# A first layer's opening with its modulation loaded, computed and used in two halves of the channels

## The reference, cut to what matters

```python
mod_l = (silu(c) @ w_mod[l] + b_mod[l])[:, None, :]
mod_c = (silu(c_ctx) @ w_mod[l] + b_mod[l])[None, None, :]
sh1, sc1, g1, sh2, sc2, g2 = split(mod_l, 6, axis=-1)
sh1c, sc1c, ... = split(mod_c, 6, axis=-1)
pl = _modulate(_rmsnorm(xl, norm1_w[l]), sh1, sc1) @ w_in[l]      # h * (1 + sc1) + sh1, then the projection
pc = _modulate(_rmsnorm(xc, norm1_w[l]), sh1c, sc1c) @ w_in[l]
```

## Time and profile before

| | |
|---|---|
| median of 3 runs | 3009.11 us (3007.6 to 3009.39) |
| profiled execution, its time | 3008.7 us |
| profiled execution, its span | 3006.9 us |
| TensorE busy | 2977.1 us (99%), 17179 matmul records |
| VectorE, ScalarE, GpSimd busy | 1657.6, 1048.0, 2075.4 us |
| mean granted TensorE clock | 0.999 of full speed |

### The profile page before, as it was taken

How to read it: one execution, slowest core, us unless ns; L and a number is a source line. 1 busy time by engine, 2 the same in 40 slices (tenths; PEclk the granted TensorE clock), 3 DMA queues, 4 the chain that set the end, 5 groups by cost and what they waited for, 6 DMA issues and landing times.

```text
span 3006.9 us, 49161 instructions
## 1 busy us (share of the span) xinstructions
PE 2977.1 (99%) x17179; PEld 2584.9 (86%) x17179; DVE 1657.6 (55%) x2214; ACT 1048.0 (35%) x1846; POOL 2075.4 (69%) x1583
## 2 busy tenths in 40 slices
PE   7999999999999999999999999999999999999999
PEld 5878978888889988887889998899888878899987
DVE  5753365889178742364347662577523652477631
ACT  4362153121146620232017650366301320166600
POOL 3614575888778887654777887788876546778874
PEclk9999999999999999999999999999999999999999
DMA  5202262322333333331223333333334313333332
GB/s 222 88 29 63 73 236 71 99 98 80 96 99 103 112 89 107 116 106 64 90 98 99 104 97 96 100 107 102 95 96 136 99 56 98 98 99 98 107 90 83
DMA packets 323100, 300.60 MB, mean 100 GB/s; under 512 B 6652, under 2 KB 316924, under 8 KB 319264
## 3 DMA queue, kind: packets, MB, share of 16 engines
q1 hardware_dynamic: 319056, 290.55, 30.5%
q10 hardware_dynamic: 3920, 8.36, 1.0%
HBM read 292.60 MB, written 2.10 MB: 98 GB/s over the span
## 4 chain that ended last, share of the span: by engine, by line
PE 96%; DVE 1%; DMA 1%; ACT 1%; issue 1%; SPq 0%; DVEq 0%; ACTq 0%
PE pm L2641 16%; PE pm L2643 16%; PE pm L2642 16%; PE pm L2770 8%; PE pm L2771 8%; PE pm L2772 8%; PE pa L2641 2%; PE pa L2643 2%; PE pa L2642 2%; PE pm L2720 1%; PE pm L2721 1%; PE pm L2722 1%; PE pm L3041 1%; DMA modraw<-in_w_mod 1%; PE pm L2671 1%; PE pa L3084 1%
## 5 line engine op out<-in xcount | busy, mean ns | idle before, releaser
L776 POOL TENSOR_TENSOR wlo<-raw,whi 128x512 fp32r<-128x512 f32 (+1 forms) x784 | 977.2, 1278 | 16.4
L772 POOL TENSOR_SCALAR whi<-raw 128x2048 fp32r<-128x2048 f32 (+1 forms) x196 | 336.5, 1717 | 699.8 <-PE pm L2643 326.5
L2641 PE MATMUL pm<-hh,whi 128*128 128x512 f32 x1064 | 421.2, 396 | 2.2 <-DVE sil L2408 2.2
L2643 PE MATMUL pm<-hh,wlo 128*128 128x512 f32 x1064 | 414.3, 389 | 0.0
L2642 PE MATMUL pm<-hl,whi 128*128 128x512 f32 x1064 | 414.3, 389 | 0.0
L794 POOL TENSOR_TENSOR wlo<-raw,whi 128x512 fp32r<-128x512 f32 x216 | 288.2, 1335 | 58.6 <-ACT whi L1445 41.1
L2770 PE MATMUL pm<-tsets,whi 128*128 128x256 f32 x1152 | 326.0, 283 | 0.0
L2771 PE MATMUL pm<-tsets,whi 128*128 128x256 f32 x1152 | 326.0, 283 | 0.0
L2772 PE MATMUL pm<-tsets,wlo 128*128 128x256 f32 x1152 | 326.0, 283 | 0.0
L2641 PE MATMUL pm<-uh,whi 128*128 128x512 f32 x836 | 325.4, 389 | 0.0
L2642 PE MATMUL pm<-ul,whi 128*128 128x512 f32 x836 | 325.2, 389 | 0.0
(11 more groups left out here) (549 smaller groups left out, 6755.0 us busy)
## 6 DMA issues: line engine op xcount, KB each, us to landing
raw<-in_w_ffn SPq DMA_DIRECT2D x88, 1024.0 KB, 5.3
raw<-in_w_in SPq DMA_DIRECT2D x61, 1024.0 KB, 5.1
raw<-in_w_ffn SPq DMA_DIRECT2D x64, 704.0 KB, 4.6
raw<-in_w_up SPq DMA_DIRECT2D x22, 1024.0 KB, 5.1
raw<-in_w_out SPq DMA_DIRECT2D x12, 1024.0 KB, 5.1
raw<-in_w_down SPq DMA_DIRECT2D x16, 704.0 KB, 4.6
modbuf<-in_w_mod SPq DMA_DIRECT2D x10, 1024.0 KB, 5.6
modraw<-in_w_mod SPq DMA_DIRECT2D x8, 1024.0 KB, 19.7
```

Of the source, the lines that this page charges most:

```text
L772: nc.gpsimd.tensor_scalar(h, r, 1.0, 1.0, ALU.mult, ALU.mult).then_inc(hi_done, 1)
L776: last = nc.gpsimd.tensor_tensor(o[:, c], r[:, c], h[:, c].bitcast(F32), ALU.subtract)
L2641: nc.tensor.matmul(out, wh, ah, start=start, stop=False)
L2643: return nc.tensor.matmul(out, wl, ah, start=False, stop=stop)
```

## The change

The modulation's first 2048 columns are loaded in two halves. The first holds groups 0 and 2, which are shift and scale of channels 0 to 511 (tiles 0 to 3), the second groups 1 and 3. The half of a tile's load is 0.5 MB, in runs of 512 columns (2 KB) where a load before had rows of 2048 columns (8 KB). `w_first` is loaded in two halves too, tiles 0 to 3 and tiles 4 to 7. The order of the transfers is now `col`, `ident`, `x`, six first halves, first half of `w_first`, two first halves, `cx`, eight second halves, second half of `w_first`, and slab 1 without a wait. One place moves: `modraw7` lies in `whi1` where it lay in `hl`.

TensorE does groups 0 and 2 of all eight tiles (`modulation_half`), four fillers, a turn of these groups, five fillers, and slab 0's products of tiles 0 to 3. Then groups 1 and 3 of all eight tiles, with the square sum of `cx` after the sixth, their turn, and slab 0's products of tiles 4 to 7. The eight fillers ahead of the first step stay; there are none around the second turn. ScalarE copies the sums of two groups at a time, each group's 32 rows by an instruction of its own, and squares `cx` only behind `hh` of tile 3. VectorE makes bias, scales, unrounded values and `hl` of tiles 0 to 3 first, then normalizes the other four tiles and adds up the squares of `cx`, and then does the second half. `modrow` is set to zero once by GpSimd.

```diff
-MOD_GROUP = (0, 0, 0, 0, 1, 1, 2, 3)
+MOD_GROUP = (0, 0, 0, 0, 0, 0, 1, 1, 2, 2, 2, 2, 2, 2, 3, 3)
+FIRST_GROUP, FIRST_K = 1, 4
...
+def mod_arrivals(b):
+
+    return 16 * (MOD_GROUP.count(b) + (b == FIRST_GROUP))
...
+            wm = io["w_mod"][0].rearrange("(k p) n -> k p n", p=P)
+
+            def mod_columns_of(half, k):
+
+                for_half = [a.rearrange("p (e h c) -> p h e c", e=2, h=2)[:, half] for a in (modraw[k][:], wm[k][:, 0:MOD_W])]
+                sp.dma_start(*for_half).then_inc(mod_loaded[MOD_GROUP[KD * half + k]], 16)
+
+            first_w = raw[0][:].rearrange("p k n -> p (k n)")
+            for k in range(KD):
+                if k == KD - 2:
+                    sp.dma_start(first_w[:, 0:FIRST_K * SLAB], io["w_first"][:, 0:FIRST_K * SLAB]).then_inc(mod_loaded[FIRST_GROUP], 16)
+                mod_columns_of(0, k)
             sp.dma_start(cx[:].rearrange("p k t -> p (k t)"), io["ctxT"]).then_inc(ctx_loaded, 16)
-
-            wm = io["w_mod"][0].rearrange("(k p) n -> k p n", p=P)
             for k in range(KD):
-                sp.dma_start(modraw[k][:], wm[k][:, 0:MOD_W]).then_inc(mod_loaded[MOD_GROUP[k]], 16)
-            sp.dma_start(raw[0][:].rearrange("p k n -> p (k n)"), io["w_first"]).then_inc(raw_loaded[0], 16)
+                mod_columns_of(1, k)
+            sp.dma_start(first_w[:, FIRST_K * SLAB:], io["w_first"][:, FIRST_K * SLAB:]).then_inc(raw_loaded[0], 16)
...
-                if i == 1:
-                    sp.wait_ge(raw_loaded[0], 16)
...
-                pool.wait_ge(raw_loaded[0], 16)
+                pool.wait_ge(mod_loaded[FIRST_GROUP], mod_arrivals(FIRST_GROUP))
                 for i, (k0, k1) in enumerate(FIRST_PIECES):
+                    if k0 == FIRST_K:
+                        pool.wait_ge(raw_loaded[0], 16)
...
+                squares(0)
+                roots(0)
+                act.wait_ge(mod_step, 2)
+                for g in (0, 2):
+                    rows = slice(32 * g, 32 * g + 32)
+                    nc.scalar.activation(modrow[0][rows, :], pm[1][rows, 0, :], ACT.Copy).then_inc(mod_step, 1)
+                act.wait_ge(mod_done, 3)
+                highs(0, 0, FIRST_K)
+                squares(1)
+                act.wait_ge(mod_used, KD)
+                for g in (1, 3):
+                    rows = slice(32 * g, 32 * g + 32)
+                    nc.scalar.activation(modrow[0][rows, :], pm[1][rows, 0, :], ACT.Copy).then_inc(mod_step if g == 1 else mod_row, 1)
+                roots(1)
+                act.wait_ge(mod_done, 6)
+                highs(0, FIRST_K, KD)
+                act.wait_ge(hn_done, KD // 2)
+                highs(1, 0, KD)
...
+                square_sums(0)
+                normalized(0, 0, FIRST_K)
+                v.wait_ge(mod_step, 5)
+                mod_columns_made(0)
+                lows(0, 0, FIRST_K)
+                normalized(0, FIRST_K, KD)
+                square_sums(1)
+                v.wait_ge(mod_turned, 1)
+                mod_columns_made(1)
+                v.sem_inc(pm_free[1], 1)
+                lows(0, FIRST_K, KD)
+                normalized(1, 0, KD)
+                lows(1, 0, KD)
...
-                    for g in range(4):
+                    for g in range(4) if i >= KD else (1, 3):
                         last = nc.tensor.matmul(out[32 * g:32 * g + 32, :], silc[:, k, :], src[:, T * g:T * g + T], start=k == 0, stop=k == KD - 1)
...
+            def modulation_half():
+
+                for k in range(KD):
+                    pe.wait_ge(mod_loaded[MOD_GROUP[k]], mod_arrivals(MOD_GROUP[k]))
+                    for g in (0, 2):
+                        last = nc.tensor.matmul(pm[1][32 * g:32 * g + 32, 0, :], silc[:, k, :], modraw[k][:, T * g:T * g + T], start=k == 0, stop=k == KD - 1)
+                last.then_inc(mod_step, 1)
+
+            def half_turn(half, bank, done):
+
+                which = ident[:].rearrange("p (g c) -> p g c", g=4)[:, half::2, 0:2]
+                for t in range(4):
+                    last = nc.tensor.matmul(bank[:, 8 * t:8 * t + 8].rearrange("p (g j) -> p g j", g=4)[:, half::2, :], modrow[0][:, P * t:P * t + P], which, start=True, stop=True)
+                last.then_inc(done, 1)
...
                 square_sum(0, std, T)
                 idle(8)
-                pe.wait_ge(mod_in, 1)
+                pe.wait_ge(mod_step, 1)
+                modulation_half()
+                idle(4)
+                pe.wait_ge(mod_step, 4)
+                half_turn(0, pm[1][:, 1, :], mod_step)
+                idle(5)
+                slab_opening(0, FIRST_K)
                 for k, _ in enumerate(modulation(0, KD)):
-                    if k == 3:
+                    if k == 5:
                         square_sum(1, rstd, CT)
-                    if k == 6:
-                        idle(4)
+                pe.wait_ge(mod_step, 6)
                 pe.wait_ge(mod_row, 1)
-                mod_turn(modrow[0], pm[1][:, 1, :])
-                idle(5)
+                half_turn(1, pm[1][:, 1, :], mod_turned)
```

More of the change, by code:

```diff
@@ L196, in build @@
         TILE = 4 * T
-        modraw = [place(f"modraw{k}", [P, MOD_W], F32, arena + (12 + 4 * k) * TILE if k < 7 else raw_at - 8 * TILE) for k in range(KD)]
+        modraw = [place(f"modraw{k}", [P, MOD_W], F32, arena + (12 + 4 * k) * TILE if k < 7 else raw_at + 12 * TILE) for k in range(KD)]
         uh = place("uh", [P, KF, T], F32R)
@@ L1033, in first, with squares @@
                 nc.scalar.preload_act_table_set("natural_log_exp_and_others")
-                for n, (src, loaded, w) in enumerate(((x, x_loaded, T), (cx, ctx_loaded, CT))):
+                def squares(n):
+                    src, loaded, w = ((x, x_loaded, T), (cx, ctx_loaded, CT))[n]
                     act.wait_ge(loaded, 16)
@@ L1040, in first, with roots @@
                         nc.scalar.activation(sqs[m % 4][:, 0:w], src[:, k, :], ACT.Square).then_inc(sq_done, 1)
-                for n, (acc, w) in enumerate(((std, T), (rstd, CT))):
+                def roots(n):
+                    acc, w = ((std, T), (rstd, CT))[n]
                     act.wait_ge(sq_summed, n + 1)
@@ L1045, in first, with highs @@
                     nc.scalar.activation(pa[n][:, 0:w], acc[:, 0:w], ACT.Exp, scale=-0.5).then_inc(rstd_done, 1)
[L1046 to L1053, removed]
+                def highs(n, k0, k1):
+                    src, hi, w = ((xn, hh, T), (cx, ch, CT))[n]
+                    for k in range(k0, k1):
+                        act.wait_ge(xn_done, KD * n + k + 1)
                         nc.scalar.activation(hi[:, k, :], src[:, k, :], ACT.Identity, bias=mod_col(0, k, n), scale=wsc[:, n, k:k + 1]).then_inc(hh_done, 1)
@@ L2044, in first, with square_sums @@
                 lower_bounds()
-                for n, (acc, w) in enumerate(((std, T), (rstd, CT))):
+                def square_sums(n):
+                    acc, w = ((std, T), (rstd, CT))[n]
                     for k in range(KD):
@@ L2054, in first, with normalized @@
                             nc.vector.tensor_copy(acc[:, 0:w], sqs[m % 4][:, 0:w]).then_inc(sq_added, 1)
-                for n, (src, dst, w) in enumerate(((x, xn, T), (cx, cx, CT))):
+                def normalized(n, k0, k1):
+                    src, dst, w = ((x, xn, T), (cx, cx, CT))[n]
                     v.wait_ge(rstd_done, n + 1)
-                    for k in range(KD):
+                    for k in range(k0, k1):
                         nc.vector.tensor_tensor(dst[:, k, :], src[:, k, :], pa[n][:, 0:w], ALU.mult).then_inc(xn_done, 1)
-                v.wait_ge(mod_turned, 1)
@@ L2061, in first @@
[L2061 to L2073, removed]
+                def mod_columns_made(half):
+                    to, bias = mod_turned_to(0)
+                    turned = mod_columns(pm[1][:, 1, :])
+                    raised = pm[1][:, 1, 4 * MOD_TILES1:5 * MOD_TILES1]
+                    at, scaled, ks = slice(half, half + 1), slice(2 + half, 3 + half), slice(FIRST_K * half, FIRST_K * half + FIRST_K)
+                    nc.vector.tensor_tensor(raised.rearrange("p (j g t) -> p t g j", g=2, t=4)[:, :, at, :], turned[:, :, scaled, :], bias[:, :, scaled, :], ALU.add).then_inc(mod_done, 1)
+                    nc.vector.tensor_tensor(to[:, :, at, :], turned[:, :, at, :], bias[:, :, at, :], ALU.add).then_inc(mod_done, 1)
+                    v.wait_ge(mod_done, 3 * half + 2)
+                    gain = cols("norm1", 0, KD).rearrange("p (o k) -> p o k", o=1)[:, :, ks].to_broadcast([P, 2, FIRST_K])
+                    nc.vector.scalar_tensor_tensor(wsc[:, 0:2, ks], raised.rearrange("p (j k) -> p j k", j=2)[:, :, ks], 1.0, gain, ALU.add, ALU.mult).then_inc(mod_done, 1)
+                    v.wait_ge(mod_done, 3 * half + 3)
@@ L2074, in first, with lows @@
+                def lows(n, k0, k1):
+                    src, hi, lo, w = ((xn, hh, hl, T), (cx, ch, cl, CT))[n]
+                    v.wait_ge(xn_done, KD * n + k1)
```

(11 more changed lines are left out.)

16 lines of the change are left out of this document (9 added, 7 removed).

## The result

The changed kernel takes 3017.36 us (median of 9 runs, 3016.7 to 3019.02) against 3008.76 for the kernel before (9 runs, 3007.35 to 3009.52): the ratio is 1.003, with a 95% interval of 1.002 to 1.004. The forecast was 3017.3. The profiled execution has a span of 3015.6 us, 8.7 more than before.

The account below looks back on a forecast made before the run. It took TensorE's matmul stream behind a serial opening as the bound, so slab 0's end counts: +6.5 us plus 1.7 for a clock drop, +8.2 on 3009.1, gives 3017.3 us; range 3012.5 to 3020.5.

Parts of the forecast that it names:

- eight steps with two groups: TensorE's first modulation half: a two-group step lasts 0.86 us like one with four, 7.05 us plus 0.25.
- slab 0 done, one drop of the clock: First projection's slab 0 ends 8.2 us later: +6.5 us, plus 1.7 for one clock drop behind the second turn; chance 50%.
- convolution starts on VectorE: VectorE reaches the convolution at 64.3 us, before its operands are needed at 69.
- the in-order wait of the second half: TensorE starts the second modulation half at 40.1 us, after tiles 0 to 3's products, though data landed at 35 to 38.
- the serial tail counted twice: Copies 1.25, turn 1.1, VectorE 0.5 and first `hh` 0.95 us recur after the second half, 47.9 to 51.7.
- The 0.25 us for a slow start of the steps: Time added to the first eight modulation steps on TensorE for the slower clock at their start.
- It just fits: VectorE's context square sums end at 45.2 us, when TensorE's sixth second-half step ends at 45.3, so no wait.
- two drops of the clock and none: Rival A: both turns lose the clock, 3019.0 us, chance 15%; or neither does, 3015.6 us, chance 12%.
- D: Rival: slab 2's bank or the context operands are late, TensorE waits 1 to 3 us more: 3018 to 3020; chance 8%.
- the 1 us of the sum: Slack for slab 2's bank: the convolution's first set ends at 74.1 us, slab 1 is through at 75 to 77.
- B: Rival: a two-group modulation step takes 0.43 us, half of four; 3011.3 to 3013.0 us; chance 12%.
- C: Rival: the opening follows its loads, slab 0 ends at 48.3 us, 2.4 us faster: 3006.7; chance 3%.

Follow-up runs that it names:

- the experiment with four groups: The changed kernel with its second half computing all four column groups again, twice the matmuls: 3018.01 us.
- the run with all edits: The changed kernel with two channel tiles per step, `x` normalized before the first turn, later context square sum, five fillers behind the second turn, four ahead: 3005.17 us.
- three more fillers: The kernel before with three more filler matmuls between the last modulation step and the turn: 3007.50 us.
- the run with two tiles to a step: The changed kernel with even and odd channel tiles in neighbouring column groups, all four working in both halves, the turn adding the sums: 3014.92 us.
- the run with half loads: The kernel before with each of the eight modulation loads issued as two transfers of half the columns, 2 KB runs: 3009.49 us.

## Why the prediction was right

The time was 3017.36 us where 3017.3 was said, and the range held it. The steps one by one, forecast and profile:

| step | forecast us | profile after us |
|---|---|---|
| first modulation step | 23.55 | 22.88 |
| eight steps with two groups | 7.05 + 0.25 | 7.06 |
| first product | 34.7 | 33.77 |
| second block of steps | 40.1 | 39.42 |
| square sum of the context | 45.3, no wait | 45.92, after a wait of 1.16 |
| last step done | 47.9 | 48.5 |
| first product of tile 4 | 51.7 | 52.35 |
| slab 0 done, one drop of the clock | 58.8 | 59.58 |
| convolution starts on VectorE | 64.3 | 64.64 |

The step that carries the result, that a step with two column groups lasts as long as one with four, held to 0.01 us over eight steps, and the experiment with four groups shows it apart from all else. So did the in-order wait of the second half, the serial tail counted twice, and the one drop of the clock. Several terms were off and partly offset each other:

- The first step came 0.7 us earlier. The fillers took 2.58 us and not 3.62. The fence below this list, from the view by tile, gives the minimum, median and maximum of their records in ns, first for the kernel before and then for the changed one. The granted clock reads 1.00 in both stretches, so the rows do not say why the pace differs. It is no effect of the change: with the same fillers this part took from 2.46 to 3.62 us in the variants' profiles.
- The 0.25 us for a slow start of the steps did not come.
- The context's sums took 5.7 us and not 4.0: their durations came from a stretch in which GpSimd stood idle, and here it did not. "It just fits" was the step that was wrong, mis-sized by the wait of 1.2 us.
- Four tiles' products took 5.65 us each time at the full clock and not 5.4, and the drop 1.6 and not 1.7.
- SyncE had not issued everything by 11.65 us, which was the reason given for its costing nothing: with twice the transfers its last issue of this group ends at 28.25. It cost nothing even so, since the data of tiles 4 to 7 were there at 38.5, within the forecast's 36 to 39.3.

```profile
L3209 PE MATMUL pm<-ident x16: 421/421/422, 19.9 to 23.1; 128*128 128x128 f32 x16
L3290 PE MATMUL pm<-ident x16: 275/275/421, 20.4 to 22.7; 128*128 128x128 f32 x16
```

The whole is 8.9 us at slab 0, 8.7 in the span and 8.6 in the medians, where the sum had 8.2. That the forecast time was met to 0.1 us is therefore luck: the rise was 0.4 us larger than forecast, and the kernel before, taken at 3009.11, had a median of 3008.76 in this comparison.

Of the rivals, two drops of the clock and none did not come: the first turn kept it, with TensorE at work nearly without a break from 20.37 on, and the second lost it. D did not come either: the convolution left slab 0's bank at 74.4 and slab 2's first matmul started at 77.47, 3.1 us later, more slack than the 1 us of the sum. The range's lower end, 3012.5, is called the upper end of B, which B itself puts at 3013.0; nothing hangs on it here. C is close to what the change would have been with the array full: the run with all edits took 3005.17, where C was put at 3006.7. For the change as written C did not come, and for the reason given, that TensorE has the modulation to do.

Open is what the split into halves is worth by itself. The best version holds both the split and edits that an unsplit opening could use as well, such as `cx` loaded last and better covered turns; such a version was not tried. Open too is in how many executions of the kernel before the clock falls, which would say why three more fillers gain 1.4 us in the profile and 0.5 in the medians.

## What to carry to other kernels

Splitting a piece of work in time to start its consumer earlier is free only if the halves together cost what the whole did: four column groups side by side are one pass, and two of them are one pass as well, so halving by groups doubled TensorE's work on the modulation, from some 7 us to 14.3 (7.06, 5.34 and 1.91), in a stretch in which the other engines waited for it. Halve along a dimension that leaves the array full, or fill the idle groups with the next tile and add the sums in a matmul that is there anyway. When an in-order engine is given a second serial tail (copy, turn, scale), count the whole tail twice, the clock behind it too, and look at what else stands between the halves on each engine's list.

## What the runs showed of the hardware

- A step of four 32-column float32 matmuls of 512 columns and one of two both last 0.86 us; four of them with two different stationary operands also go side by side (3.66 us for four such steps).
- An idle stretch can cost TensorE twice. In the run with two tiles to a step a wait of 4.21 us was followed by the lower clock from 44 to 54 us: its first product of tile 4 came 3.2 us earlier than in the changed kernel (49.18 for 52.35), but the time was only 2.4 us less. Five fillers on each side of the turn kept the clock at 1.00 in the three profiles that had them.
- The granted clock of a window does not always tell TensorE's pace: ahead of the first modulation step it reads 1.00 while filler records last 421 ns, against 275 behind the first turn.
- VectorE's addition of 128x256 with both inputs in SBUF lasted 1.31 us instead of 0.42 beside GpSimd's subtraction of 128x512. Its subtractions with one input in PSUM were not slowed beside the same GpSimd work: two took 1.36 us in the kernel before, and 1.36 in the changed kernel at 36.48, where GpSimd stood idle.
- Loads ran at 420 to 428 GB/s in rows of 8 KB (the kernel before, 16 to 32 us) and at 386 to 391 in runs of 2 KB (the run with half loads, the same stretch).
